# Decoder trunk on one core: weight copy with one input, renewal on VectorE alone, output tiles paired by k step, rings of 3 and 2 blocks

## The reference, cut to what matters

```python
def squared_relu_mlp(x, w_up, w_down):
    h = jax.nn.relu(x @ w_up)
    return (h * h) @ w_down

def rmsnorm(x, g):
    y = x * lax.rsqrt(jnp.mean(x * x, axis=-1, keepdims=True) + RMS_EPS)
    return y * g

# each of the four sub-layers:  h = h + norm_post(f(norm_pre(h)))
```

## Time and profile before

| | before |
|---|---|
| profiled execution, own time | 1827.72 us |
| its span on the core | 1825.9 us |
| median of 3 runs | 1827.74 us |
| mean granted TensorE clock | 0.923 |
| PE busy | 1577.9 us (86%) |
| POOL busy | 1332.7 us (73%) |
| DVE busy | 1266.2 us (69%) |
| ACT busy | 469.1 us (26%) |
| DMA | 27.4% of 16 engines' span, mean 87 GB/s |

### The profile page before, as it was taken

How to read it: one execution, slowest core, us unless ns; L and a number is a source line. 1 busy time by engine, 2 the same in 40 slices (tenths; PEclk the granted TensorE clock), 3 DMA queues, 4 the chain that set the end, 5 groups by cost and what they waited for, 6 DMA issues and landing times.

```text
span 1825.9 us, 29727 instructions
## 1 busy us (share of the span) xinstructions
PE 1577.9 (86%) x11978; PEld 1479.8 (81%) x11978; DVE 1266.2 (69%) x1075; ACT 469.1 (26%) x1158; POOL 1332.7 (73%) x586
## 2 busy tenths in 40 slices
PE   5999888876499699999997699976769799999995
PEld 5999656876489699999997599953349799999995
DVE  6899888799941698018845936998862996038645
ACT  3433322555621321002100311125542321002100
POOL 5878588556568789888887766644418788888885
PEclk8999999988699799999999799978879799999997
DMA  4222000244423133333333123442212133323321
GB/s 146 75 83 85 18 6 12 105 173 150 150 58 92 47 91 86 92 89 92 92 93 104 45 60 116 135 179 93 70 47 81 47 92 91 92 87 91 92 90 47
DMA packets 44151, 159.40 MB, mean 87 GB/s; under 512 B 5026, under 2 KB 5410, under 8 KB 43810
## 3 DMA queue, kind: packets, MB, share of 16 engines
q1 hardware_dynamic: 44066, 158.25, 27.4%
HBM read 142.07 MB, written 16.16 MB: 87 GB/s over the span
## 4 chain that ended last, share of the span: by engine, by line
PE 55%; DVE 32%; issue 6%; ACT 3%; POOL 2%; DMA 1%; SPq 0%; DVEq 0%; POOLq 0%; ACTq 0%
PE GP L495 17%; PE GP L497 17%; PE GP L496 17%; DVE cacc L1274 4%; DVE hT L1376 2%; DVE acc L1396 2%; DVE hc L1336 2%; DVE hs L1333 2%; DVE kq L1473 1%; DVE aL L1371 1%; DVE hs L1330 1%; DVE decay L1293 1%; DVE misc L1517 1%; DVE hst L1305 1%; DVE yss L1337 1%
## 5 line engine op out<-in xcount | busy, mean ns | idle before, releaser
L405 POOL TENSOR_TENSOR wH<-wraw,cst 128x1024 fp32r<-128x1024 f32 x216 | 532.7, 2466 | 325.6 <-PE GP L497 315.4
L495 PE MATMUL GP<-aH,wH 128*128 128x260 f32 x1920 | 559.9, 292 | 89.4 <-DVE aL L1371 35.2
L409 POOL TENSOR_TENSOR wL<-wraw,wH 128x1024 fp32r<-128x1024 f32 x216 | 576.4, 2668 | 17.0
L497 PE MATMUL GP<-aH,wL 128*128 128x260 f32 x1920 | 553.5, 288 | 0.0
L496 PE MATMUL GP<-aL,wH 128*128 128x260 f32 x1920 | 552.8, 288 | 0.0
L495 PEld LDWEIGHTS GP<-aH,wH 128*128 128x128 f32 x1920 | 373.3, 194 | 98.3 <-issue 49.6
L495 PE MATMUL GP<-hidH,wH 128*128 128x260 f32 x1536 | 440.8, 287 | 8.0 <-DVE hidL L1347 7.3
L497 PE MATMUL GP<-hidH,wL 128*128 128x260 f32 x1536 | 435.9, 284 | 0.0
L496 PE MATMUL GP<-hidL,wH 128*128 128x260 f32 x1536 | 434.9, 283 | 0.0
L496 PEld LDWEIGHTS GP<-aL,wH 128*128 128x128 f32 x1920 | 373.8, 195 | 0.1
L497 PEld LDWEIGHTS GP<-aH,wL 128*128 128x128 f32 x1920 | 373.4, 194 | 0.0
(11 more groups left out here) (255 smaller groups left out, 2041.9 us busy)
## 6 DMA issues: line engine op xcount, KB each, us to landing
wraw<-wblk SPq DMA_DIRECT2D x216, 512.0 KB, 3.6
hs<-ssm_in SPq DMA_DIRECT2D x16, 512.0 KB, 3.7
sssm<-hs SPq DMA_DIRECT2D x16, 512.0 KB, 2.8
ktile<-kcache SPq DMA_DIRECT2D x16, 512.0 KB, 3.6
vtile<-vcache SPq DMA_DIRECT2D x16, 512.0 KB, 4.5
hT<-x_t SPq DMA_DIRECT2D x4, 520.0 KB, 5.1
kt_out<-kT SPq DMA_DIRECT2D x1, 2080.0 KB, 6.6
vt_out<-vT SPq DMA_DIRECT2D x1, 2080.0 KB, 10.6
```

Source lines behind the costliest of these rows:

```text
L405: pool.tensor_tensor(wH[:, d, :].rearrange("p (k n) -> p k n", k=8), raw[:, s, :].rearrange("p (k n) -> p k n", k=8), cst[:, C_ONE:C_ONE + ...
L409: pool.tensor_tensor(wL[:, d, :], raw[:, s, :], wH[:, d, :].bitcast(F32), ALU.subtract).then_inc(w_lo, 1)
L495: pe.matmul(out, lh, rh, start=first, stop=False)
L497: return pe.matmul(out, ll, rh, start=False, stop=last)
```

## The change

Five edits:

- The high half of a weight block is a copy of the block by `tensor_copy`, which has one input, instead of a product with ones. The low half stays.
- POOL no longer scales the sub-layer's output. DVE does (`scaled`): fT = fT * gpost * rpost, one tile ahead of the sum hT = hT + fT. Renewal and low half are thus three DVE operations to a tile instead of two, with none on POOL.
- `tile_pair`: where a GEMM of one block to a tile takes its input by k steps and nothing is called after each tile (xbc, up0a, q, o, up1a), its first two output tiles go through the k steps together, 12 matmuls to a step, into both pairs of banks.
- RAW is 2 instead of 4, SPL 3 instead of 2. Both rings together take as much SBUF as before. The places in SP's list at which it turns from the weights to other transfers (zb, kb, ob) are the block's number plus RAW, and so move two blocks earlier.
- The loops of SP, POOL and TensorE over blocks and tiles are written out.

```diff
-RAW, SPL = 4, 2
+RAW, SPL = 2, 3
...
     @block.gpsimd
     def _(pool):
-        def split(i, s, first):
...
-            pool.tensor_tensor(wH[:, d, :].rearrange("p (k n) -> p k n", k=8),
-                               raw[:, s, :].rearrange("p (k n) -> p k n", k=8),
-                               cst[:, C_ONE:C_ONE + 1, :].broadcast_to([P, 8, P]), ALU.mult).then_inc(w_hi, 1)
...
+        def split(b):
+            s, d = b % RAW, b % SPL
+            pool.wait_ge(raw_in[s], 16 * (b // RAW + 1))
+            if b >= SPL:
+                pool.wait_ge(blk, b + 1 - SPL)
+            pool.tensor_copy(wH[:, d, :], raw[:, s, :]).then_inc(w_hi, 1)
+            pool.wait_ge(w_hi, b + 1)
             pool.tensor_tensor(wL[:, d, :], raw[:, s, :], wH[:, d, :].bitcast(F32), ALU.subtract).then_inc(w_lo, 1)
...
-        def scale_output(p):
-
-            pool.wait_ge(rp_s, p + 1)
-            for m in range(KT):
-                pool.tensor_tensor(fT[:, m, :], fT[:, m, :], rpost[:, :], ALU.mult).then_inc(fr_s, 1)
...
+        def tile_pair(name, inH, inL, each_k):
+
+            m, b = TILE0[name], BLOCK0[name]
+            if m >= 2:
+                pe.wait_ge(taken, m)
+            pe.wait_ge(w_lo, b + 2)
+            for k in range(8):
+                each_k(k)
+                for u in range(2):
+                    ins = block_k(m + u, b + u, 0, k, 1, inH, inL)
+                    if k == 7:
+                        ins.then_inc(blk, 1)
...
             a, e = tiles or (0, n)
-            if a == 0:
-                one(0, each_k)
-                one(1)
+            if a == 0 and each_k is not None and BLOCKS[name] == 1:
+                tile_pair(name, inH, inL, each_k)
                 a = 2
...
+            def scaled(m):
+                STT(fT[:, m, :], fT[:, m, :], pc(gpost, m), rpost[:, :], ALU.mult, ALU.mult).then_inc(fr_s, 1)
+
+            v.wait_ge(rp_s, p + 1)
+            scaled(0)
             for m in range(KT):
+                if m + 1 < KT:
+                    scaled(m + 1)
                 v.wait_ge(fr_s, 8 * p + m + 1)
-                STT(hT[:, m, :], fT[:, m, :], pc(gpost, m), hT[:, m, :], ALU.mult, ALU.add).then_inc(h_n, 1)
+                TT(hT[:, m, :], hT[:, m, :], fT[:, m, :], ALU.add).then_inc(h_n, 1)
                 if m and p < 3:
                     lows(m - 1)
```

More of the change, by code:

```diff
@@ L80, in build @@
     O_H, O_A, O_HID, O_Y, O_F = 0, 16640, 49920, 116480, 149760
-    O_RAW, O_SPL, O_SM = 166400, 182784, 199168
+    O_RAW, O_SPL, O_SM = 166400, 166400 + 4096 * RAW, 199168
     hT = at("hT", [P, KT, T], O_H)
@@ L317, in stream @@
         def stream(a, b):
[L318 to L322, removed]
+            for b in range(a, b):
+                sp.wait_ge(w_lo, b + 1 - RAW)
+                sp.dma_start(raw[:, b % RAW, :], wblk[b, :, :]).then_inc(raw_in[b % RAW], 16)
         zb, kb, ob = BLOCK0["z"] + RAW, BLOCK0["q"] + RAW, BLOCK0["o"] + RAW
@@ L398, in _ @@
     def _(pool):
-        def split(i, s, first):
[L400 to L403, removed]
-            pool.tensor_tensor(wH[:, d, :].rearrange("p (k n) -> p k n", k=8),
-                               raw[:, s, :].rearrange("p (k n) -> p k n", k=8),
-                               cst[:, C_ONE:C_ONE + 1, :].broadcast_to([P, 8, P]), ALU.mult).then_inc(w_hi, 1)
-            pool.wait_ge(w_hi, i * RAW + (s + 1))
+        def split(b):
[5 more added lines that the diff above has]
+            pool.wait_ge(w_hi, b + 1)
             pool.tensor_tensor(wL[:, d, :], raw[:, s, :], wH[:, d, :].bitcast(F32), ALU.subtract).then_inc(w_lo, 1)
@@ L412, in stream @@
         def stream(a, b):
[L414 to L424, removed]
-            for j in range(a, b):
-                split(j // RAW, j % RAW, False)
-        def scale_output(p):
-            pool.wait_ge(rp_s, p + 1)
-            for m in range(KT):
-                pool.tensor_tensor(fT[:, m, :], fT[:, m, :], rpost[:, :], ALU.mult).then_inc(fr_s, 1)
+            for j in range(a, b):
+                split(j)
         stream(0, SPL)
@@ L473, in _ @@
             at_ = BLOCK0[nxt] + SPL
-            scale_output(p)
             if p == 1:
-                stream(at_, BLOCK0["o"] + SPL)
-                at_ = BLOCK0["o"] + SPL
+                stream(at_, BLOCK0["o"] + RAW)
+                at_ = BLOCK0["o"] + RAW
                 pool.wait_ge(sa_s, 1)
@@ L488, in _ @@
         stream(at_, NBLK)
-        scale_output(3)
     @block.tensor
@@ L497, in three, with block_k, tile @@
             return pe.matmul(out, ll, rh, start=False, stop=last)
[L499 to L504, removed]
+        def block_k(m, b, kb, k, nk, inH, inL):
+            kk, d, par = kb * 8 + k, b % SPL, m % 2
+            lh, ll = wH[:, d, k * P:(k + 1) * P], wL[:, d, k * P:(k + 1) * P]
+            for h in range(2):
+                ins = three(G[2 * par + h][:, 0:HALF], lh, ll, inH[:, kk, HV[h]], inL[:, kk, HV[h]],
+                            kk == 0, kk == nk * 8 - 1)
+            return ins
+        def tile(name, t, inH, inL, each_k=None):
+            nk, m = BLOCKS[name], TILE0[name] + t
+            if m >= 2:
+                pe.wait_ge(taken, m - 1)
             for kb in range(nk):
-                d = (b[1] + kb) % SPL
-                pe.wait_ge(w_lo, b[0] + kb + 1)
+                b = BLOCK0[name] + t * nk + kb
+                pe.wait_ge(w_lo, b + 1)
                 for k in range(8):
@@ L510, in tile @@
                         each_k(kb * 8 + k)
[L511 to L516, removed]
-                ins.then_inc(blk, 1)
+                    ins = block_k(m, b, kb, k, nk, inH, inL)
+                ins.then_inc(blk, 1)
+        def tile_pair(name, inH, inL, each_k):
+            m, b = TILE0[name], BLOCK0[name]
+            if m >= 2:
+                pe.wait_ge(taken, m)
[6 more added lines that the diff above has]
+                        ins.then_inc(blk, 1)
         def gemm(name, inH, inL, after=None, each_k=None, tiles=None, inside=None):
             n = dict((a, b) for a, b, _ in GEMMS)[name]
-            nk, m0, b0 = BLOCKS[name], TILE0[name], BLOCK0[name]
-            def one(m, hook=None):
-                tile(name, (m0 + m, (m0 + m) % 2), (b0 + m * nk, b0 + m * nk), inH, inL, m0 + m >= 2, hook)
             if after is not None:
-                for m in range(n):
-                    one(m, each_k if m == 0 else inside and (lambda k, m=m: inside(m, k)))
-                    after(m)
+                for t in range(n):
+                    tile(name, t, inH, inL, each_k if t == 0 else inside and (lambda k, t=t: inside(t, k)))
+                    after(t)
                 return
             a, e = tiles or (0, n)
-            if a == 0:
-                one(0, each_k)
-                one(1)
+            if a == 0 and each_k is not None and BLOCKS[name] == 1:
+                tile_pair(name, inH, inL, each_k)
                 a = 2
[L537 to L540, removed]
+            for t in range(a, e):
+                tile(name, t, inH, inL, each_k if t == 0 else None)
         pe.wait_ge(in_one, 16)
```

## The result

The changed kernel took 1747.79 us (median of 4 runs, 1745.73 to 1749.89) against 1827.93 us of the kernel before on the same chip: a ratio of 0.9563, with a 95% interval of 0.9544 to 0.9583. The direction and most mechanisms were as forecast. The sizes of the copy's terms were not, and a rise of TensorE's granted clock where its waits went was no term of the sum.

The account below looks back on a forecast made before the run. TensorE was taken to bound the steady MLP stretch, DVE, held up by POOL, z and the renewals; z -14, xbc -6, p = 0 and 2 -12, p = 1 -10, end -3.2, costs +1 sum to -44: 1783 us, range 1767 to 1811.

Parts of the forecast that it names:

- The price of the copy: POOL's high half of each weight block: 1.2 us as a copy instead of 2.47 as a product, 1.2 saved a block.
- the paired tiles: Renewals p = 0 and 2: both first tiles end together at 625.8, tile 2 starting at 626.7 instead of 633.8; -6 each.
- the end: Last renewal, p = 3: sixteen DVE operations of 0.67 us from rpost, 10.7 us, without POOL's scaling; -3.2 us.
- xbc: -8 of 10: TensorE's waits of 6.1 and 3.9 us shrink by 8; first pair costs +2; sum -6, between +2 and -10.
- I take 70%: z stage: 17 splits, each copy blocking DVE 1.2 us less, 20 us at most; 70% taken, -14 us.
- p = 1, "-10": Renewal p = 1: renewal 3.2 us earlier, four shorter splits 4.8, two additions before rpost 2; sum -10 us.
- the attention (+1.5): One block more to split beside the attention's tail, on DVE: +1.5 us; shorter copies in v tiles take back 1.5.
- o's pair (+1): Pairing o's first two tiles costs +1 us for the handover and saves nothing, as per-head work is slower than TensorE.
- the slow copy: Rival: the copy on POOL takes as long as the product, 2.47 us; total 1811 us; chance 0.13.
- POOL as the bound: Rival: the copy is slower than the product and POOL becomes the bound; at 3.6 us, 1887 us total; chance 0.07.
- Loads just in time: Rival: two raw slots make the z loads late; z gives 0 to -4, total 1795 us; chance 0.10.
- The half clock: Rival: TensorE stays at half clock in the pairs, no gain at p = 0 and 2; total 1795 us; chance 0.10.

Follow-up runs that it names:

- the last three kernels above: Changed kernel with the third split behind the additions of squares (1745.66 us), behind POOL's products at start and out (1745.33), or both with xbc not paired (1741.01).

## Why the prediction was wrong

The price of the copy (1.2 forecast, 1.11 measured), DVE's pace of 0.67 us, the first k step, the paired tiles, the end and the untouched MLP stretch were right, and p = 1's mechanism too. Three terms, all of them the copy's, failed, and each of them was too small.

The Trainium skill ("GPSIMD Engine Reference", section 3.1) gives 1.03 cycles an element for a short body that its ports bound and about 1.8 for a tight loop. The prediction's estimate from these, 0.9 to 1.5 us, held: the trace has 1.11.

- *"xbc: -8 of 10", "sum -6".* This step failed in its mechanism. It took TensorE's waits as the most that could be had. Of the 10 us, 5.0 of the 6.1 in the stage went, and the 3.9 at the scan's start stayed 3.9. What the sum put at nothing is TensorE's own busy time: 4.7 us less with the same matmuls, at a granted clock of 0.98 in place of 0.96. The stage alone measured -10.3, with the copy alone -12.2, and the pair costs 1.5 of the difference (151.8 us in the run without pairs). The other 5.5 of the row's 15.8 lie in the scan (139.9 to 134.4), which the forecast had at nothing too. They are not settled: the scan took 134.4 to 136.8 us in most kernels with the copy, but 140.5 in two, at a granted clock of 0.91.
- *"I take 70%"* for z. Of the 17 x 1.36 = 23.1 us by which the copies are shorter, z's own tiles gained 22.8, with the copy alone 22.3: nearly all, and above even the bound of 20. The operations take turns, so nearly the whole difference arrives at DVE while DVE has work. The granted clock rose from 0.83 to 0.93 in that stretch; whether this adds to the gain no run separates.
- *p = 1, "-10"*: -14.8, of which the copy alone gives 9.0 where its share was 4.8. The K/V low halves and the additions behind them are 7.7 shorter, not 4.8, and TensorE's busy time in q falls by 2.0 with the clock, which was no term.

The costs charged to the attention (+1.5) and to o's pair (+1) did not come: -5.5 and 0. The +1.5 was for a third block of o split ahead of the attention's tail, which is not in the change: POOL splits two there in both kernels (`BLOCK0["o"] + SPL` with SPL = 2 before, `BLOCK0["o"] + RAW` with RAW = 2 after). The -5.5 has no settled cause. That stretch read 151.3 to 158.0 us in the traces of the changed kernel and the last three kernels above, which issue the same work in it, so a difference of some 5 us there is no evidence for any edit.

Of the rivals, the slow copy and POOL as the bound are refuted by the 1.11 us. Loads just in time happened as described, but cost at most 2 us instead of z's 14. The half clock held for the first 5.7 us of the pair only.

Last, the sum took the parts as independent. By the medians the copy alone gives 58 and the rest 7; together they give 80. The traces show the renewals gaining 8 more together, as at p = 1, where the wait at the sum of squares stays 9.5 us without the copy whatever the renewal gains ahead of it. They also show 9 lost elsewhere, so that for most of the 15 us the place stays open.

## What to carry to other kernels

Before sizing a shorter operation by the waits it causes on the bound engine, take the busy time of every engine in that stretch, and the granted clock. An engine without slack (DVE's 94% here, in xbc and in z) passes on nearly the whole saving, until the next engine's own work, here TensorE's 152 us, stops it. And TensorE's waits are not the most that can be had: its own busy time fell with them, by 4.7 us in xbc. Where two engines take turns by whole operations, shorten the operation of the one that has slack; it is the other one that gets faster. And when a ring gains a slot, look at what stands behind the extra fill in the filling engine's queue.

## What the runs showed of the hardware

A GpSimd copy of 128x1024 from fp32 to fp32r took 1.04 us undisturbed and 1.11 in the mean, against 2.39 and 2.47 for the product of the same tile with a broadcast column: 0.43 of it, less than half. It held VectorE's two-input operations up as the product does, until its end (2.05 us in place of 1.22). TensorE's granted clock read 0.83 in the 10 us behind a wait of 2.4 us, and the same behind one of 3.7, in stretches in which it was busy throughout.
